# The opening of a two-layer encoder trunk: the input in five pieces on two queues, and products interleaved with transposes one by one

## The reference

```python
def rmsnorm(x, w):
    xf = x.astype(jnp.float32)
    y = xf * lax.rsqrt(jnp.mean(xf * xf, axis=-1, keepdims=True) + EPS)
    return (y * w.astype(jnp.float32)).astype(x.dtype)

def even_layer(x, norm_w, w_in, w_out, ...):
    h = rmsnorm(x, norm_w)
    proj = jnp.einsum('bsd,de->bse', h, w_in)
    qa, ka, va, ga, qh, ffw, fbw, ih, gh = split_cols(proj, EVEN_SIZES)
    ...
```

## Time and profile before

| what | value |
|---|---|
| median of 3 runs | 1120.28 us (1118.6 to 1120.28) |
| the profiled execution, its own time | 1120.19 us |
| the profiled execution, its span | 1118.4 us |
| TensorE busy | 98% of the span |
| mean granted clock of TensorE | 0.997 |

### The profile page before, as it was taken

One profiled execution on the slowest core, in us unless ns is written; L12 is line 12 of the kernel. 1 busy time (PEld: TensorE's weight loads), 2 busy tenths in 40 slices (PEclk: granted clock), 3 DMA queues, 4 the chain that ended last, 5 costly groups with the idle time before them and its releaser, 6 DMA issues. The chain is left out here.

```text
span 1118.4 us, 18504 instructions
## 1 busy us (share of the span) xinstructions
PE 1091.8 (98%) x5690; PEld 911.2 (81%) x5690; DVE 967.7 (87%) x1956; ACT 679.4 (61%) x1311; POOL 0.2 (0%) x4
## 2 busy tenths in 40 slices
PE   8999999999999999999999999999999999999996
PEld 7778778878888888888888867887888888888875
DVE  6879889889889889889889888889888888988886
ACT  6475565565654654654654665376677666677764
POOL 0000000000000000000000000000000000000000
PEclk9999999999999999999999999999999999999999
DMA  8614423323324224224225120554332324323111
GB/s 231 170 38 111 135 76 79 110 75 91 97 75 101 87 75 114 74 75 126 61 75 145 44 76 22 125 144 112 97 94 56 94 62 123 100 73 94 57 39 76
DMA packets 132634, 103.67 MB, mean 93 GB/s; under 512 B 5488, under 2 KB 118512, under 8 KB 132592
## 3 DMA queue, kind: packets, MB, share of 16 engines
q1 hardware_dynamic: 131760, 102.28, 33.4%
q10 hardware_dynamic: 832, 0.85, 0.2%
HBM read 77.95 MB, written 2.10 MB: 72 GB/s over the span
## 5 line engine op out<-in xcount | busy, mean ns | idle before, releaser
L75 PE MATMUL bank_proj<-hH,w_hi 128*128 128x512 f32 x856 | 341.5, 399 | 1.1 <-DVE w_lo L1323 1.1
L77 PE MATMUL bank_proj<-hH,w_lo 128*128 128x512 f32 x856 | 334.4, 391 | 0.0
L76 PE MATMUL bank_proj<-hL,w_hi 128*128 128x512 f32 x856 | 334.2, 390 | 0.0
L77 PEld LDWEIGHTS bank_proj<-hH,w_lo 128*128 128x128 f32 x856 | 160.8, 188 | 34.9
L75 PEld LDWEIGHTS bank_proj<-hH,w_hi 128*128 128x128 f32 x856 | 161.2, 188 | 32.2 <-DVE w_lo L1323 1.9
L76 PEld LDWEIGHTS bank_proj<-hL,w_hi 128*128 128x128 f32 x856 | 161.2, 188 | 30.0 <-issue 0.2
L2088 ACT ACTIVATE probs<-probs,small 128x256 f32<-128x256 f32 (+1 forms) x128 | 70.9, 556 | 52.2 <-DVE small L2347 51.9
L1323 DVE TENSOR_TENSOR w_lo<-w_raw,w_hi 128x1024 fp32r<-128x1024 f32 x73 | 88.4, 1218 | 0.9 <-ACT w_hi L789 0.9
L2095 ACT ACTIVATE probsT<-bank_odd_turn 128x256 fp32r<-128x256 f32 (+1 forms) x128 | 48.8, 433 | 64.7 <-PE bank_odd_turn L1811 64.2
L789 ACT ACTIVATE w_hi<-w_raw 128x1024 fp32r<-128x1024 f32 x73 | 76.9, 1053 | 0.2
L854 ACT ACTIVATE probs<-bank_score,small 128x512 f32<-128x512 f32 x64 | 43.4, 684 | 49.5 <-DVE small L1146 41.6
(11 more groups left out here) (462 smaller groups left out, 2157.4 us busy)
## 6 DMA issues: line engine op xcount, KB each, us to landing
w_raw<-in_w_in_even SPq DMA_DIRECT2D x71, 512.0 KB, 4.8
w_raw<-in_w_in_odd SPq DMA_DIRECT2D x36, 512.0 KB, 4.9
qs<-parts SPq DMA_DIRECT2D x96, 128.0 KB, 2.3
ks<-parts SPq DMA_DIRECT2D x40, 256.0 KB, 4.3
o_raw<-in_w_out_even SPq DMA_DIRECT2D x15, 512.0 KB, 6.3
o_raw<-in_w_out_odd SPq DMA_DIRECT2D x14, 512.0 KB, 6.5
mixT<-in_x SPq DMA_DIRECT2D x4, 256.0 KB, 6.2
rope<-in_rope SPq DMA_DIRECT2D x2, 512.0 KB, 7.4
```

The lines of the kernel that those rows point to most:

```text
L75: pe.matmul(out, hi, moving_hi, start=start, stop=False)
L76: pe.matmul(out, hi, moving_lo, start=False, stop=False)
L77: return pe.matmul(out, lo, moving_hi, start=False, stop=stop)
```

## The change

The input comes in five pieces of one, one, two, two and two feature tiles. SyncE's queue loads tokens 0 to 255 of all five and tokens 256 to 511 of the last; ScalarE's queue loads tokens 256 to 511 of the first four, with `eye` behind the first. The 9 warming matmuls become 7 ahead of the first turn, 2 ahead of the second and 4 ahead of the third. TensorE turns three tiles instead of four ahead of the first product, and from there on does one product and one turn in alternation until tile 7 is turned behind the fifth product. ScalarE and VectorE split tiles 1 to 3 before the second half of the first weights; keeping tiles 0 and 1 of `xT` moves behind that.

```diff
-WARM = 9
+WARM = (7, 2, 4)
+PIECES = ((0, 1), (1, 2), (2, 4), (4, 6), (6, 8))
...
-        x_landed = [sem(f"x_landed{i}", unit=DMA) for i in range(4)]
+        x_landed = [sem(f"x_landed{i}", unit=DMA) for i in range(len(PIECES))]
...
             def load_x(a, i):
-                part = x[2 * a * P:2 * (a + 1) * P, 2 * i * P:2 * (i + 1) * P].rearrange("(t p) d -> p t d", p=P)
-                sp.dma_start(x_tiles[a][:, :, 2 * i * P:2 * (i + 1) * P], part).then_inc(x_landed[i].sem, DMA)
+                cols = slice(PIECES[i][0] * P, PIECES[i][1] * P)
+                part = x[2 * a * P:2 * (a + 1) * P, cols].rearrange("(t p) d -> p t d", p=P)
+                sp.dma_start(x_tiles[a][:, :, cols], part).then_inc(x_landed[i].sem, DMA)
...
             load_half(0, half_landed)
             load_x(0, 1)
+            load_x(0, 2)
             load_half(4, w_in_sem[0])
-            for i in (2, 3):
-                for a in range(2):
-                    load_x(a, i)
+            load_x(0, 3)
+            load_x(0, 4)
+            load_x(1, 4)
             load(0, -1)
...
-                if k % 2 == 0:
-                    pe.wait_ge(x_landed[k // 2].sem, x_landed[k // 2].at(0, 2))
+                for i, (first, _) in enumerate(PIECES):
+                    if k == first:
+                        pe.wait_ge(x_landed[i].sem, x_landed[i].at(0, 2))
...
-            for c in range(WARM):
-                pe.matmul(PB[1][:, 0:P], ones, ones, start=True, stop=True)
-            for k in range(4):
+            for k in range(3):
+                for c in range(WARM[k]):
+                    pe.matmul(PB[1][:, 0:P], ones, ones, start=True, stop=True)
                 turn_x(k)
...
-            proj(0, -2, 0, 1)
-            turn_x(4)
-            turn_x(5)
-            proj(0, -2, 1, 2)
-            turn_x(6)
-            proj(0, -2, 2, 3)
-            turn_x(7)
-            proj(0, -2, 3, 4)
-            proj(0, -2, 4)
+            for k in range(5):
+                proj(0, -2, k, k + 1)
+                turn_x(k + 3)
+            proj(0, -2, 5)
...
-            for i in range(2):
-                part = x[2 * P:4 * P, 2 * i * P:2 * (i + 1) * P].rearrange("(t p) d -> p t d", p=P)
-                act.dma_start(x_tiles[1][:, :, 2 * i * P:2 * (i + 1) * P], part).then_inc(x_landed[i].sem, DMA)
+            for i in range(4):
+                cols = slice(PIECES[i][0] * P, PIECES[i][1] * P)
+                part = x[2 * P:4 * P, cols].rearrange("(t p) d -> p t d", p=P)
+                act.dma_start(x_tiles[1][:, :, cols], part).then_inc(x_landed[i].sem, DMA)
...
-            high_x(1)
+            for k in range(1, 4):
+                high_x(k)
             act.wait_ge(w_in_sem[0].sem, w_in_sem[0].at(0, 0))
             act.activation(w_hi[0][:, 4:KT], w_raw[0][:, 4:KT], ACT.Copy).then_inc(w_high.sem, 1)
             keep_first_x()
-            for k in range(2, KT):
+            for k in range(4, KT):
                 high_x(k)
...
-            low_x(1)
+            for k in range(1, 4):
+                low_x(k)
             dve.wait_ge(w_high.sem, w_high.at(0, -2))
             dve.tensor_tensor(w_lo[0][:, 4:KT], w_raw[0][:, 4:KT], w_hi[0][:, 4:KT].bitcast(F32),
                               ALU.subtract).then_inc(w_low.sem, 1)
+            low_x(4)
             keep_x(KEPT[0])
-            for k in range(2, KT):
+            for k in range(5, KT):
                 low_x(k)
```

More of the change, by code:

```diff
@@ L943, in _ @@
             for t, into in enumerate((decay, soft, turned, probs)):
-                for i in range(4):
-                    act.wait_ge(x_landed[i].sem, x_landed[i].at(0, 2))
+                for landed_piece in x_landed:
+                    act.wait_ge(landed_piece.sem, landed_piece.at(0, 2))
                 act.activation(into[:, :, :].rearrange("p a t -> p (a t)"), x_tiles[t // 2][:, t % 2, :], ACT.Square,
```

## The result

The changed kernel takes 1122.45 us in the median of 18 runs, the kernel before 1119.65 us in the median of its 18 on the same chip; the ratio is 1.0024, 95% interval 1.0017 to 1.0030 (one disturbed execution of each, at 1725 and 6254 us, is left out of it). So it is slower, by 2.8 us in the medians of all 18 and by 3.2 in those of the other 17, where no change was forecast, and 1122.45 lies above the range. The lowest runs are 1119.85 after and 1117.91 before. Those 17 of the kernel before fall in two groups, nine from 1117.91 to 1119.30 and seven from 1120.01 to 1120.46, with one at 1122.25; of those of the changed kernel three lie from 1119.85 to 1120.80, one at 1121.30 and thirteen from 1122.01 to 1123.73. The profiled execution after took 1122.04 us with a span of 1120.3, against 1120.19 and 1118.4.

A forecast was written before the change was run, and what follows sets the result against it. TensorE bounds the kernel, its opening hanging on tile 7's turn. That turn 0.15 us later, less a margin of about 0.1, rounded up to +0.1, gave 1120.19 + 0.1 = 1120.3 us; range 1118.5 to 1122.2.

The forecast's parts named there:

- What bounds it: Opening: TensorE is 98% busy, but everything after 15 us hangs on when tile 7 is turned; margin about 0.1 us.
- Landing and warming: Opening: first turn at 4.3 us, tile 1 landing at 7.2 (bounds 6.7 and 8.0), warming to 8.5, tile 2 at 8.9.
- D: How much later tile 7 is turned in the opening: 14.65 for 14.47 us, taken as +0.15 or so.
- the alternation: Opening, tile 2's turn to tile 7's: five product-and-turn pairs, 5.65 us, plus 0.1 for the first product after a pause.
- the old stall: TensorE's wait at 30.38 us for the low part behind the root and rotation; forecast to shift by +0.1 us.
- the sum's base: The profiled execution's 1120.19 us, to which the shift of 0.1 was added; taken to stand for the median, 1120.28.
- drops further on: Clock drops past the opening: no term in the sum; rows were read as showing no fall after waits of 1.5 us.
- The clock: Opening: idle pieces of 1.6 and 0.4 us replace one of 2.6; clock taken to stay at the upper level.
- The first: Rival: clock falls in the opening all the same, tile 7 at 16.0, D +1.5, 1121.7 us; chance 0.28.
- the second: Rival: low clock lasts through the alternation, 11.8 to 15.2 us, costing 1.55 more, 1123.2 us; chance 0.08.
- The third, faster one: Rival: pieces land sooner, tile 7 turned near 13.8, -0.75, 1119.4 us; tile 6 not before about 12.6; chance 0.12.

The follow-up runs named there:

- experiment 5: Kernel before with nine more warming matmuls between the turns of tiles 1 and 2, filling the opening's idle stretch: 1119.15 us, ratio to before 0.9996.
- experiment 7: Kernel before with nine warming matmuls in the opening's idle stretch and seven in the second head's wait: 1118.72 us, ratio to before 0.9994.
- 6: Changed kernel with ten warming matmuls instead of two between its first two turns: 1121.10 us, ratio to the kernel before 1.0012.
- 8: Changed kernel with ten warming matmuls between its first two turns and seven in the second head's wait: 1120.42 us, ratio to before 1.0003.
- 4: Changed kernel with tiles 5 and 6 turned behind the second product and tile 7 behind the third: 1121.33 us, ratio to before 1.0009.
- 1: Kernel before run once more, no edit: 1120.39 us, ratio 1.0004.
- 2: Kernel before with only the change's pieces and two queues; order, splits and nine warming matmuls as before: 1120.42 us, ratio 1.0001.
- experiment 3: Kernel before with only the change's order of turns, products and splits; pieces, queues and warming as before: 1121.49 us.
- 9: Changed kernel with the turns of tiles 5 to 7 drawn forward and ten warming matmuls between its first two turns: 1120.62 us, ratio to before 1.0008.
- 10: Change's pieces and queues with before's order, and ten warming matmuls between the first two turns: 1119.37 us, ratio to before 0.9994.
- 11: Change's order with before's pieces and queues, and nine warming matmuls ahead of the turn of tile 2: 1120.34 us, ratio to before 1.0009.

## Why the prediction was wrong, point by point

**What bounds it** held as far as the second head: TensorE's shift at 30.85 (0.47) is 0.44 at 124, and the opening hangs on the turn of tile 7 and the low part of the second weights, which made TensorE idle before 18.70 as foreseen.

**Landing and warming.** Seven warming matmuls and the first turn came at 4.39 for 4.3. Tile 1 landed at 7.85, near the upper bound of 8.0, not at 7.2. The four warming matmuls are queued behind it, ended at 9.3 and held the turn of tile 2 until 9.32 (8.9 was forecast). From there the alternation took 5.80 us to tile 7, forecast 5.75. So D was 0.65, not 0.15; the term of D that was mis-sized is the landing of tile 1, and what stands behind its wait. Forecast shift at the old stall +0.1, measured +0.47.

**The steps that failed** are two, both on the clock. The first is the sum's base: "That execution lies 0.09 below the median of 1120.28, so the same stands for the median." In that execution the clock had dropped in the opening. The prediction priced that drop itself, at 1.5 us, and then took a profile with it as the kernel. The three runs shown ahead of it already had one at 1118.6, and over 17 executions the lower group is the larger. With the clock up the same order turns tile 7 at 12.97 (experiment 5) or 14.00 (experiment 7), the changed kernel with its hole filled at 15.39 or 15.13 (6 and 8), and the medians of these pairs lie 1.95 and 1.70 us apart. That is why a forecast of no change failed. It is not why the time lies above the range, for the base was too high and not too low.

The second step is that drops further on were put at nothing: the sum has no term for them, on the reading of the earlier trace rows that a wait of 1.5 us leaves the clock up. In the profiled execution of the changed kernel the drop behind such a wait cost 1.60 us, most of the 1.87 between the spans. With that wait and the opening's filled, the changed kernel ran at 1120.42 on another chip, near the forecast of 1120.3, which had such drops left out.

**The clock.** The forecast that it stays up in the opening came true in the profiled execution, and tile 7 was turned late all the same, with five products ahead of it. The Trainium skill, "TensorE: Matmul & The Clock Gate", section "Part 4: PE-mode transpose", would have had tile 1's turn hold nothing; the clock stayed at 1.00 across it, with warming matmuls on either side, so the trace does not decide that rule. The inference from the earlier trace rows, that a wait of 1.5 us does not bring the clock down, was wrong: behind the same wait of the second head it fell in the profiles of the changed kernel and of experiments 4 and 6, and not in those of before and of experiments 1, 2, 3, 5, 9, 10 and 11. Nor does a longer wait always bring it down, as the 3.65 us of experiment 3 show. The same page of the Trainium skill, "Part 1: The HAM clock gate", says that one kernel has more or fewer slow matmuls at its start from run to run. The profiles agree for the start: the first turn took 0.41 us in the profile of before and 0.59 in that of experiment 1, the same kernel.

**The rivals.** The first (the clock falls in the opening, 1121.7) and the second (it stays low, 1123.2) put drops in the opening only; drops further on are what was missing. In the profile of the changed kernel the first did not happen; whether it did in others of its executions is not shown. The third, faster one took the last piece for the limit, tile 6 not before 12.6. Experiment 5 turned tile 6 at 11.83, so in that execution the limit did not stand.

**Open.** Why the clock falls behind the wait of the second head in one execution and not in another is not shown, nor whether the changed kernel's executions have more drops by its nature. Thirteen of its 17 lie above 1122 us, with its hole filled four of 12, though its one profile has no drop in the opening and the filling turned no tile earlier. Drops in the opening of other executions would fit; only one was profiled.

## What to carry to other kernels

Set a forecast against the state that the profiled execution was in: if a drop of the clock stands in the very stretch that is changed, work the sum out for the stretch without it too, and look whether the runs shown already fall in groups. In this opening, where one engine turns tiles and another splits them, an earlier first product won nothing; products put between the turns delayed the last turn, and with it everything that needs all tiles. Times that differ by a few tenths of a us need more than one profile of each kernel: the landing of a piece and the waits differ from execution to execution too.

## What the runs showed of the hardware that was not expected

The place where TensorE falls to the lower clock changes from one execution to the next: the opening, near 126, near 656 and near 761 us, behind single waits of 1.5 to 2.6 us or two of 0.8 and 0.9. The waits behind the opening were followed by 1.00 in the profiles of other executions, and so was one of 3.65 us in the opening of experiment 3. A drop cost about 1.5 us in the opening (two turns and a product in 3.04 us at 0.50, and 1.57 at 1.00) and 1.6 near 126. Filling two such places with warming matmuls brought 9 of 12 executions of the kernel before within 1.0 us (1118.03 to 1118.99); the profile of one of the other three has its drops at two places that were not filled.
